# Input projections of two mixers from float32r high and low parts, in eighths of a chunk, in a two-layer float32 kernel

## What is computed

```python
# layer 0: mLSTM and gated linear attention, both in chunks of 64 tokens
mq, mk, mv, mi, mf, mo, gq, gk, gv, glr, gr = split_cols(x @ w_in, EVEN_SPLITS)
qk = silu(causal_depthwise_conv(concat([mq, mk]), conv_w))
hm = head_rms_norm(mlstm_chunked(...), g) * sigmoid(mo)
hg = head_rms_norm(gla_chunked(...), g) * silu(gr)
y  = concat([hm, hg]) @ w_out
# layer 1: attention over the keys that an indexer picks (top 64)
q, k, v, qi, ki, wi = split_cols(x @ w_in, ODD_SPLITS)      # then rotary, top-k, softmax
y  = attention(...) @ w_out
```

## Time and profile before

| | us |
|---|---|
| median of 3 runs | 1947.81 |
| the profiled execution, its own time | 1946.26 |
| its span, first to last instruction | 1944.4 |
| PE busy in the span | 1737.1 (89%) |
| DVE busy | 510.5 (26%) |
| ACT busy | 281.1 (14%) |
| data read from HBM, over the span | 275 GB/s |

### The profile page before, as it was taken

How to read it: one execution, slowest core, us unless ns; L and a number is a source line. 1 busy time by engine, 2 the same in 40 slices (tenths; PEclk the granted TensorE clock), 3 DMA queues, 4 the chain that set the end, 5 groups by cost and what they waited for, 6 DMA issues and landing times.

```text
span 1944.4 us, 16738 instructions
## 1 busy us (share of the span) xinstructions
PE 1737.1 (89%) x6855; PEld 893.1 (46%) x6855; DVE 510.5 (26%) x979; ACT 281.1 (14%) x471; POOL 18.5 (1%) x36
## 2 busy tenths in 40 slices
PE   7999999989899888898869999988989988889984
PEld 5884444467543324433234454446764332443321
DVE  2301011435621111211160071233562111121115
ACT  1012011333210000100010001133321000010000
POOL 1000000000000000000000000000000000000000
PEclk9999999999899999999978999998989999999997
DMA  6444343274489999999972334325448999999994
GB/s 229 147 162 141 130 162 111 103 276 169 175 360 422 421 422 421 421 421 421 422 299 86 130 115 145 130 87 211 178 174 356 423 421 422 421 418 421 421 421 207
DMA packets 121425, 535.86 MB, mean 276 GB/s; under 512 B 12949, under 2 KB 13049, under 8 KB 70665
## 3 DMA queue, kind: packets, MB, share of 16 engines
q1 hardware_dynamic: 120776, 530.62, 68.7%
q0 software_dynamic: 576, 4.19, 0.5%
HBM read 532.70 MB, written 2.10 MB: 275 GB/s over the span
## 4 chain that ended last, share of the span: by engine, by line
PE 57%; issue 27%; DMA 8%; DVE 5%; ACT 2%; SPq 1%; POOL 0%; POOLq 0%; DVEq 0%
PE ps L684 23%; PE ps L914 8%; PE ps L666 6%; PE ps L968 4%; DMA ring<-in_moe_w_down 4%; DMA ring<-in_moe_w_up 3%; PE ps L706 3%; PE ps L708 3%; PE ps L707 3%; PE ps L636 1%; DMA arena<-in_moe_w_up 1%; PE ps L894 1%; PE ps L895 1%; PE ps L1064 1%; DVE w_lo L1593 1%
## 5 line engine op out<-in xcount | busy, mean ns | idle before, releaser
L684 PE MATMUL ps<-ring,hT 128*128 128x512 f32 x1024 | 443.3, 594 | 0.0
L684 PEld LDWEIGHTS ps<-ring,hT 128*128 128x128 f32 x1024 | 194.8, 191 | 240.8 <-issue 240.5
L1805 DVE TENSOR_TENSOR arena<-ps,arena 128x512 f32<-128x512 f32 x128 | 82.9, 685 | 409.5 <-PE ps L904 409.5
L914 PE MATMUL ps<-arena,hT 128*64 128x512 f32 x768 | 176.6, 615 | 8.3 <-issue 5.0
L968 PE MATMUL ps<-ring,arena 128*64 128x512 f32 x768 | 170.0, 594 | 10.5 <-DMA ring<-in_moe_w_down 10.5
L914 PE MATMUL ps<-arena 128*64 128x512 f32 x512 | 114.7, 596 | 21.5 <-DMA arena<-in_moe_w_up 9.3
L914 PE MATMUL ps<-ring,arena 128*64 128x512 f32 x512 | 114.7, 597 | 10.3 <-DMA ring<-in_moe_w_up 6.2
L968 PEld LDWEIGHTS ps<-ring,arena 128*64 128x64 f32 x768 | 55.9, 137 | 121.9 <-issue 99.4
L914 PEld LDWEIGHTS ps<-arena,hT 128*64 128x64 f32 x768 | 56.4, 142 | 119.0 <-issue 116.3
L666 PE MATMUL ps<-hT,ring 128*128 128x256 f32 x512 | 110.8, 380 | 0.0
L1272 ACT ACTIVATE y_hi<-ps 128x512 fp32r<-128x512 f32 x64 | 36.5, 596 | 497.6 <-PE ps L904 261.9
(11 more groups left out here) (304 smaller groups left out, 1436.0 us busy)
## 6 DMA issues: line engine op xcount, KB each, us to landing
arena<-in_moe_w_gate SPq DMA_DIRECT2D x48, 2048.0 KB, 18.3
ring<-in_moe_w_down SPq DMA_DIRECT2D x48, 2048.0 KB, 20.5
arena<-in_moe_w_up SPq DMA_DIRECT2D x32, 2048.0 KB, 20.7
ring<-in_moe_w_up SPq DMA_DIRECT2D x32, 2048.0 KB, 20.0
ring<-in_ab_w_in SPq DMA_DIRECT2D x24, 2048.0 KB, 8.0
ring<-in_moe_w_gate SPq DMA_DIRECT2D x16, 2048.0 KB, 20.2
arena<-in_moe_w_down SPq DMA_DIRECT2D x16, 2048.0 KB, 19.4
ring<-in_c_w_in SPq DMA_DIRECT2D x16, 2048.0 KB, 8.0
```

The source lines that it names most:

```text
L684: last = nc.tensor.matmul(tile(stage, i)[:, :], hT[:, 8 * u + k, tt * P:(tt + 1) * P], w[:, k, :], start=(u + k == 0), stop=(u == 1 and k ...
L914: last = nc.tensor.matmul(ps[bank][e * CAP:(e + 1) * CAP, :], xc(k)[:, at:at + CAP], w[:, e, kk, :], start=(k == 0), stop=(k == KT - 1), s ...
L1805: v.tensor_tensor(d, ps[6 + tt][:, :], d, ALU.add).then_inc(s["drained"][tt], 1)
```

## The change

All 20 input chunks are computed as the output projection was: float32r high and low parts, three matmuls each. The weights of input and output projection form one stream of units, each an eighth of a chunk (128 x 1024, 0.5 MB), through 8 raw slots (low parts in place) and 4 slots of high parts, all in what was the ring. `chunk_transposed` is gone: chunks 0 to 3 of layer 0 come out with tokens on partitions, are copied (`natural`) and turned by PE (`turn`). The two narrow projections are made by `narrow` from 128 (padded) columns. The order of the layer 0 chunks and of the mixer steps is new: each step stands a chunk later than its operands. The angles are computed at the start of the program; their Sin stands before ACT's first copies of x. The four units of the first half of output chunk 0 of layer 1 run before `heads_out(2)` into tiles of their own (`out1_0a`). The last transposes of layer 0 go in four quads between units of the output projection. x is loaded into `mix` first and again into h later.

```diff
-L0_CHUNKS = [MQ, MK, GQC, GK, MV, MV + 512, MO, MO + 512, GV, GV + 512, GR, GR + 512]
+L0_CHUNKS = [MQ, MK, GQC, GK, MV, MV + 512, GV, GV + 512, MO, MO + 512, GR, GR + 512]
+RAW, HIGH = 8, 4
...
+            def load_unit(lay, n):
+                if n >= RAW:
+                    wait_unit_used(sp, lay, n - RAW)
+                elif lay == 1:
+                    wait_last_pair(9 + n // 4)
+                sp.dma_start(raw_unit(n)[0].rearrange("p (k n) -> p k n", k=2), unit_source(lay, n)).then_inc(unit_loaded[n % RAW], 16)
...
+            for n in range(4):
+                load_unit(0, n)
             sp.dma_start(w2[0:RANK, :], a["ab_gla_gate_w2"][0]).then_inc(small_loaded, 16)
...
+            for n in range(4, RAW):
+                load_unit(0, n)
             sp.dma_start(norm_g[:, 0:1024], ...).then_inc(small_loaded, 16)
             sp.dma_start(norm_g[:, 1024:2048], ...).then_inc(small_loaded, 16)
...
+            def unit(lay, n, hi, lo):
+                c, e = n // 8, n % 8
+                stage = chunk_stage(lay, c, e)
+                opens = e == 0 or (ends_tiles(lay, n - 1) if n else True)
+                pe.wait_ge(w_lo_ready, (UNITS[0] if lay == 1 else 0) + n + 1)
...
+                for tt in range(TT):
+                    for k in range(2):
+                        nc.tensor.matmul(t, x_h, w_l[:, k, :], start=(opens and k == 0), stop=False)
+                        nc.tensor.matmul(t, x_h, w_h[:, k, :], start=False, stop=False)
+                        last = nc.tensor.matmul(t, x_l, w_h[:, k, :], ...)
...
+            def narrow(stage, hi, w_l, w_h, lo):
+                t = tile(stage)[:, 0:SEQ]
+                for k in range(KT):
+                    nc.tensor.matmul(t, w_l[:, k, :], hi[:, k, :], start=(k == 0), stop=False)
+                    nc.tensor.matmul(t, w_h[:, k, :], hi[:, k, :], start=False, stop=False)
+                    last = nc.tensor.matmul(t, w_h[:, k, :], lo[:, k, :], start=False, stop=(k == KT - 1))
...
+            def turn(c):
+                for i in range(2):
+                    transposes(f"turn{c}", i, [nat[:, c % 2, tt, j * P:(j + 1) * P] for j in (2 * i, 2 * i + 1) for tt in range(TT)])
...
 # PE, layer 0
+            narrow("gates", x_hi, ws_lo0, ws_hi0, x_lo0); chunk(0, 0); decay
+            chunk(0, 1); turn(0); gcols, rsums; chunk(0, 2); turn(1); chunk(0, 3); turn(2)
+            chunk(0, 4); turn(3); chunk(0, 5); mlstm_scores(0)
+            chunk(0, 6); mlstm_out(0); mlstm_scores(1); chunk(0, 7); mlstm_out(1); mlstm_scores(2); kend
+            chunk(0, 8); mlstm_out(2); mlstm_scores(3); gstate; chunk(0, 9); mlstm_out(3); gattn
+            chunk(0, 10); gO; chunk(0, 11); mixed_quad(0..2); out_units(0, 0, ...) with mixed_quad(3) inside
...
 # PE, layer 1: as before with chunk for chunk_natural, and
+            heads_in(3)
+            pe.wait_ge(attn_lo_ready, 2)
+            out_units(1, 0, 0, 4)
+            heads_out(2)
+            heads_out(3)
+            pe.wait_ge(attn_lo_ready, KVH)
+            out_units(1, 0, 4, 8)
...
 # ACT
+            def high_parts(lay, *units):
+                for n in units:
+                    if n >= HIGH:
+                        wait_unit_used(act, lay, n - HIGH)
+                    act.wait_ge(unit_loaded[n % RAW], ...)
+                    act.activation(high_unit(n), raw_unit(n)[0], ACT.Copy).then_inc(w_hi_ready, 1)
...
+            three DMAs of the gate columns, after POOL's memset of w_small0
+            act.wait_ge(trig_in, 1)
+            act.activation(sinv..., kf[:, 0, :], ACT.Sin); act.activation(cosv..., ACT.Sin)
+            tokens_hi("xT0", range(8), x_hi_ready)
+            act.activation(ws_hi0[:, :, :], w_small0[:, :, :], ACT.Copy).then_inc(gate_hi_ready, 1)
+            high_parts(0, *range(4))
...
 # DVE
+            def low_parts(lay, *units):
+                for n in units:
+                    v.wait_ge(w_hi_ready, lay * UNITS[0] + n + 1)
+                    v.tensor_tensor(lo, raw, high_unit(n).bitcast(FP32), ALU.subtract).then_inc(w_lo_ready, 1)
...
+            v.wait_ge(small_loaded, 16 * 12)
+            (the angles, as before) .then_inc(trig_in, 1)
+            tokens_lo("xT0", range(8), x_lo0, x_hi_ready)
+            v.tensor_tensor(ws_lo0, w_small0, ws_hi0, ALU.subtract).then_inc(gate_lo_ready, 1)
+            low_parts(0, *range(4)); (gates) low_parts(0, 4..11); (router columns, decay) low_parts(0, 12..19)
+            conv(0); low_parts(0, 20..27); (la scan) conv(1); low_parts(0, 28..43)
...
 # DVE, layer 1
+            tokens_lo("xT1", range(8), x_lo1, x_hi_ready, 8); ws_lo1; low_parts(1, 0..3)
...
+            (12 index tiles) low_parts(1, 28, 29); reduce_sum of tt = 1; low_parts(1, 30); reduce_sum of tt = 0; low_parts(1, 31)
+            top-k: low_parts(1, 32 + n) after each of the 8 steps
+            rope_heads(0); low_parts(1, 40..43); masked_scores(0); low_parts(1, 44, 45); normalised(0); ...
+            rope_heads(3); heads_lo(0); heads_lo(1); masked_scores(3); normalised(3)
```

More of the change, by code:

```diff
@@ L36 @@
 HALF = SLOT // 2
+UNIT = 2 * BANK
+RAW, HIGH = 8, 4
 ROWS = TAPS * 8 + 4 + 4 * KT
@@ L714, in out_chunk, with chunk, out_units @@
+            def chunk(lay, c):
+                for n in range(8 * c, 8 * c + 8):
+                    unit(lay, n, x_hi, x_lo0 if lay == 0 else x_lo1)
+            def out_units(lay, c, first_e, last_e):
+                n0 = 8 * (len(chunks[lay]) + c)
+                for e in range(first_e, last_e):
+                    unit(lay, n0 + e, x_hi, mix_lo if lay == 0 else attn_lo)
+                    if c > 0 and e == 1:
                         raw_transposes(lay, c - 1)
-                    if c > 0 and part == 1:
+                    if c > 0 and e == 3:
@@ L791, in _ @@
                 last.then_inc(psum_full, 1)
+            chunk(0, 1)
+            turn(0)
             pe.wait_ge(e_done, 1)
@@ L993, in _ @@
             wait_hT("xT1")
-            drained_before(pe, "small1", 0)
-            pe.wait_ge(small1_loaded, 16)
-            for k in range(KT):
-                last = nc.tensor.matmul(tile("small1")[0:IDH + IH, 0:SEQ], w_small1[:, k, :], hT[:, k, :],
-                                        start=(k == 0), stop=(k == KT - 1))
-            last.then_inc(psum_full, 1)
+            pe.wait_ge(gate_lo_ready, 2)
+            narrow("small1", x_hi, ws_lo1, ws_hi1, x_lo1)
             def wait_tiles(stage, n):
@@ L1125, in out_chunks @@
                     raw_tile(lay, 3, tt)
-            hT_tiles("xT0")
+            act.wait_ge(gate_w_clear, 1)
+            wr = w_in[0].rearrange("(k p) n -> p k n", p=P)
+            with nc.allow_non_contiguous_dma(reason="columns of the gates, once"):
+                for at, lo, hi in ((0, MI, MI + NH), (32, MI + NH, MI + 2 * NH), (64, GLR, GLR + RANK)):
+                    act.dma_start(w_small0[:, :, at:at + hi - lo], wr[:, :, lo:hi]).then_inc(gate_w_loaded, 16)
+            act.wait_ge(trig_in, 1)
+            act.activation(sinv[:, :, :].rearrange("p a b -> p (a b)"), kf[:, 0, :], ACT.Sin)
+            act.activation(cosv[:, :, :].rearrange("p a b -> p (a b)"), kf[:, 1, :], ACT.Sin).then_inc(trig_out, 1)
+            tokens_hi("xT0", range(8), x_hi_ready)
+            act.wait_ge(gate_w_loaded, 48)
+            act.activation(ws_hi0[:, :, :], w_small0[:, :, :], ACT.Copy).then_inc(gate_hi_ready, 1)
+            high_parts(0, *range(4))
             act.wait_ge(lf_abs, 1)
```

802 lines of the change are left out of this document (439 added, 363 removed).

## The result

The changed kernel takes 1850.07 us (median of 4 runs, 1848.36 to 1851.55) beside 1946.63 for the kernel before (4 runs of the same comparison, 1945.02 to 1948.44). The ratio is 0.9507, 95% interval 0.9495 to 0.9518: 96.6 us faster, against a predicted 83.7. The predicted 1864 lies 14 us above, the range (1848 to 1895) holds it near its low end. The profiled execution has a span of 1847.8 us.

The account below looks back on a forecast made before the run. PE was taken to bound the input projections, HBM the expert stage. Layer 0 -63.3, start +18.8, layer border -1.5 and layer 1 -37.7 make -83.7 on 1946.3: 1862.6, with 1.5 for the median 1864 us; range 1848 to 1895.

Parts of the forecast that it names:

- The chunks: 20 input chunks at 22.4 us each instead of 27.6: -62.4 us in layer 0, -41.6 in layer 1.
- Layer 0: From chunk 0 to the output projection: chunks, a stall, turns, mixer waits and output border together give -63.3 us.
- The border to the output: Before layer 0's output projection: 10.3 us become about 5.3, only first copies and transposes remain, -5.0 us.
- The supply: ACT copies and DVE subtractions for each unit keep up with PE; absences up to 8.9 us cost nothing.
- The stall of 3.6: After layer 0's chunk 2, DVE's scan block and convolution make unit 28 late: PE stands 3.6 us.
- the one of 2.5: In layer 1 chunk 3, DVE's index reductions make unit 31 late: PE stands 2.5 us.
- The start: Small loads, angles, splitting and narrow product ahead of chunk 0 move its start from 29.4 to 48.2: +18.8 us.
- The border: Between the layers, PE no longer waits for DVE's angles; narrow product 8.9 us for 10.1: -1.5 us.
- Layer 1: Chunks, a 2.5 us stall, dearer index and attention steps, and covered softmax together give -37.7 us.
- cover the softmax of head group 3: Layer 1's attention tail: four output units (11.2 us) fill PE's wait before the output projection, -11.0 us.
- The rule on transfers: Weight loads of 512 KB fall below the 1 MiB batching advice; by it 0.4 us more per unit, about 1928 us.
- Slower than before: Rival, chance 0.03: unit loads on SP's queue come one behind another, 5.1 us for each 2.8 us unit, 2232 us.

Follow-up runs that it names:

- the start: Changed kernel with the positions and the two norm gains on semaphores of their own, so the angles wait for the positions alone; 1836.62 us.
- the two blocks: Changed kernel with low parts 28 and 29 ahead of chunk 1's convolution in layer 0, and layer 1's smaller index reduction first; 1842.32 us.
- the split wait: Changed kernel with PE waiting for group 3's attention low parts only ahead of unit 70, and layer 0's mixer low parts 192 bytes further on; 1843.94 us.
- all edits together: Changed kernel with separate semaphores, low parts 28 and 29 earlier, smaller reduction first, attention wait split, mixer low parts at byte 33792; 1822.31 us.

## Why the prediction was right, and where it was not

**The chunks** carry the gain, as predicted, but a chunk takes 21.9 to 22.1 us, not 22.4. This is the term that was mis-sized. The 0.233 us was read in the output stage of before and taken as the price of a matmul; it was that price with the weights' high part at an unfavourable place, as the runs with moved operands show. 0.35 to 0.4 us on 20 chunks make some 7 to 8 of the 13 us by which the prediction was short.

**Layer 0** gained 8.2 us more than predicted (-71.5 for -63.3). The chunks with the stall give -63.9 for -58.8, although 1.9 us went to the clock; before's three chunks from 142.5 to 226.8 had also been dearer than 27.6, 84.3 us in all. The border to the output shrank from 10.4 to 4.1 us (-6.3 for -5.0), the turns cost 3.5 for 4.2, and the mixer's other steps gave -4.8 for -3.7.

**The supply** held: the slack of 8.9 us covers everything but the two blocks the walk named. The stall of 3.6 was measured as 3.73 and the one of 2.5 as 2.98. What the walk left out is the clock: behind the first stall PE ran at half clock for 3.4 us, 1.9 us more.

**The start** was right in kind and in size (+17.6 for +18.8), out of three errors: the landing 3.7 later, the angles 3.2 shorter, the narrow product 1.4 shorter. The run with semaphores of their own confirms the chain.

**The border** gained 3.2 for 1.5, mostly by the narrow product, 7.2 us where 8.9 was taken.

**Layer 1** matches (-37.9 for -37.7) by errors that cancel. The step that failed is the last one: four units "cover the softmax of head group 3", -11.0. In before, the end of the last chunk (1291.0) and the output's start (1330.3) lay 39.3 us apart; after, 48.7 with 11.3 of units, so 37.4: -1.9, where the terms for this stretch (+1.5, +3.4, -11.0) make -6.1. Up to the four units it is +5.9 for +4.9, and from there -7.8 for -11.0. The shorter pitch paid for it: 2 us in the output (94.4 for 96.7), and the chunks gave -40.9 for -39.1.

Part of this miss is the clock, and so luck of the one execution. The stretch took 48.7 us at a mean of 0.86 in the changed kernel; in three other runs with the same code there (the start, the two blocks, the mixer's low parts) it took 45.0 at 0.96, by which the -1.9 would be -5.6. But the reason that the prediction gave for the -11.0 doesn't hold even so: the units stood over the softmax for 4.7 of their 11.3 us, and with them in another place the kernel takes 0.8 us more, not 9 to 11. The reasoning counted PE's idle time as room to fill, without asking when ACT would take up its part again.

**The rule on transfers** didn't bite. The 160 unit loads of 512 KB landed 3.7 us after issue in the median. The Trainium skill, DMA: Bandwidth & Descriptors, Anatomy of one DMA — SWDGE (gpsimd) path, has the fixed 2.0 us and the 436e3 from which the prediction's estimate of 3.2 us comes; its fit is for DMAs issued by GpSimd, while these are issued by SP. But the loads overlap, no wait of PE in the stream's chunks ends with a unit load, and the chunk has its 21.9 us at a DMA share of 0.59. The Trainium skill, DMA: Bandwidth & Descriptors, Bandwidth, says to batch to at least 1 MiB; here a transfer of half of that cost nothing, and the 1928 us worked out by the rule didn't come.

**Slower than before** had no sign.

## What to carry to other kernels

A rate read in one stage holds the placement of that stage's operands; compare two stages before it is carried over. An engine's idle time is room for other work only if the engines it works with can go on meanwhile: name who waits for whom before pricing a cover. Before the lengths of a half-idle stretch are compared between two executions, look at the granted clock of both. And look at what each wait counts: small loads that share a semaphore make the first consumer wait for the last of them, here for 13.4 us.

## What the runs showed of the hardware

- The pitch of float32r matmuls (128x128 by 512 columns) depends on where an operand lies: 226.7 ns where the offsets of all operands in their buffers are multiples of 256 bytes; 230.8 to 231.3 with the low part of the tokens (the operand of one matmul in three) 64 bytes or 128 bytes off; 233.3 with the high part of the weights (two in three) 64 bytes off, and 228.8 with it at 128. Why, and whether other types show it, stays open.
- In the changed kernel a wait of 3.73 us was followed by 3.4 us at half clock, a wait of 2.25 us by none. In the run with the low parts of layer 1's tokens moved, a wait of 2.24 us at the same place was followed by some 3 us at half clock: the length of the wait alone doesn't tell it.
- The tail of the attention, where PE is half idle, differs between executions of the same code: 21.3 us at a granted clock of 0.76 in the changed kernel, 17.6 at 1.00 in the run with the mixer's low parts moved, the same code there. So the split wait is compared at equal clocks: 17.2 for 21.2 us at 0.75 and 0.76, and at 1.00 it is 14.1 (all edits together) for 17.6. The window of the 17.6:

```profile
1229.00:1246.60 17.60, 8.81 (x36) 4.49 (x34) 5.37 (x6) 10.54 (x16) 1.10 (x2) 1.00 0.14 43
```

- Three transfers of single columns held ACT's queue for 13.5 us (12.1 in another run). Beside them a small broadcast held SP's queue for 7.7 us (1.0 in before, where the gathers weren't beside it); that the one slows the other wasn't tested.
